# One fused two-block transformer kernel: order and queues of its first transfers, and zeros multiplied while x is loaded

## The reference

```python
h = rms_norm(x, norm_mix[l])
z = h @ w_in[l]
zu, zv, zq, zk, zval = jnp.split(z, cuts, axis=-1)
u = jax.nn.gelu(zu, approximate=False).reshape(Bn, Sn, SGU_GROUPS, SGU_CH)
v = jax.nn.gelu(zv, approximate=False).reshape(Bn, Sn, SGU_GROUPS, SGU_CH)
```

## Time and profile before

| what | value |
|---|---|
| median of 3 runs | 1712.66 us (1711.61 to 1713.93) |
| the profiled execution's own time | 1711.31 us |
| its span, first to last instruction | 1709.5 us |
| mean granted TensorE clock | 0.987 |
| busy: PE, DVE, ACT, POOL | 1586.1, 939.8, 690.7, 32.7 us |
| HBM read | 410.27 MB, 241 GB/s over the span |
| chain that ended last, by engine | PE 68%, DMA 21%, DVE 5%, ACT 4% |

### The profile page before, as it was taken

How to read it: one execution, slowest core, us unless ns; L and a number is a source line. 1 busy time by engine, 2 the same in 40 slices (tenths; PEclk the granted TensorE clock), 3 DMA queues, 4 the chain that set the end, 5 groups by cost and what they waited for, 6 DMA issues and landing times.

```text
span 1709.5 us, 30570 instructions
## 1 busy us (share of the span) xinstructions
PE 1586.1 (93%) x12545; PEld 1279.1 (75%) x12545; DVE 939.8 (55%) x1612; ACT 690.7 (40%) x1038; POOL 32.7 (2%) x42
## 2 busy tenths in 40 slices
PE   6999999787888887999999999999999999899999
PEld 5988876554555555788888678888788889678887
DVE  4887451011111111477667867676766677667766
ACT  5556451011001100444545465445545463754543
POOL 3000000000000000000000200000000000000000
PEclk9999999999999999999999999999999999999999
DMA  9744379999999999856464625564464653236460
GB/s 296 239 155 165 129 305 427 429 428 429 429 429 429 427 429 426 310 185 209 161 218 156 173 99 182 186 203 166 148 217 162 210 173 126 73 123 213 159 217 25
DMA packets 166637, 413.00 MB, mean 242 GB/s; under 512 B 5879, under 2 KB 131148, under 8 KB 154284
## 3 DMA queue, kind: packets, MB, share of 16 engines
q1 hardware_dynamic: 164512, 407.99, 64.0%
q0 software_dynamic: 1824, 4.03, 0.8%
q10 hardware_dynamic: 236, 0.06, 0.0%
HBM read 410.27 MB, written 1.78 MB: 241 GB/s over the span
## 4 chain that ended last, share of the span: by engine, by line
PE 68%; DMA 21%; DVE 5%; ACT 4%; issue 1%; SPq 0%; DVEq 0%; ACTq 0%
DMA odd_expert<-in_w_up_dram 19%; PE bank L1290 18%; PE bank L650 10%; PE bank L651 10%; PE bank L652 10%; PE bank L1294 9%; PE bank L1043 3%; DMA odd_expert<-in_w_gate_dram 2%; PE bank L1068 1%; ACT whi L1509 1%; DVE wlo L1979 1%; DVE x L2017 1%; PE bank L664 1%; PE bank L833 1%; PE bank L1057 1%
## 5 line engine op out<-in xcount | busy, mean ns | idle before, releaser
L1290 PE MATMUL bank<-x,whi 128*128 128x512 f32 x1408 | 356.4, 393 | 1.2 <-DVE x L2017 0.9
L1290 PEld LDWEIGHTS bank<-x,whi 128*128 128x128 f32 x1408 | 255.8, 189 | 50.9 <-issue 2.0
L2520 DVE TENSOR_TENSOR wlo<-raw,whi 128x2048 fp32r<-128x2048 f32 x120 | 271.4, 2289 | 32.6 <-ACT whi L1827 27.2
L1827 ACT ACTIVATE whi<-raw 128x2048 fp32r<-128x2048 f32 x120 | 225.4, 1913 | 57.9 <-PE bank L652 57.9
L1294 PEld LDWEIGHTS bank<-x,wlo 128*128 128x128 f32 x1408 | 193.7, 190 | 13.5
L1294 PE MATMUL bank<-x,wlo 128*128 128x256 f32 x1408 | 200.8, 282 | 0.0
L1979 DVE TENSOR_TENSOR wlo<-raw,whi 128x2048 fp32r<-128x2048 f32 x67 | 154.3, 2312 | 62.8 <-ACT whi L1509 62.2
L1509 ACT ACTIVATE whi<-raw 128x2048 fp32r<-128x2048 f32 x67 | 127.0, 1908 | 35.0 <-PE bank L652 29.3
L650 PE MATMUL bank<-whi,hh_hi 128*128 128x512 f32 x352 | 138.1, 392 | 3.1 <-DVE hh_lo L2505 3.1
L651 PE MATMUL bank<-whi,hh_lo 128*128 128x512 f32 x352 | 137.5, 391 | 0.0
L652 PE MATMUL bank<-wlo,hh_hi 128*128 128x512 f32 x352 | 137.0, 389 | 0.0
(11 more groups left out here) (351 smaller groups left out, 2302.9 us busy)
## 6 DMA issues: line engine op xcount, KB each, us to landing
raw<-in_ffn_w_gate_dram SPq DMA_DIRECT2D x44, 1024.0 KB, 5.4
raw<-in_ffn_w_up_dram SPq DMA_DIRECT2D x44, 1024.0 KB, 6.6
raw<-in_ffn_w_down_dram SPq DMA_DIRECT2D x44, 1024.0 KB, 6.2
raw<-in_w_gate_dram SPq DMA_DIRECT2D x16, 2048.0 KB, 20.9
raw<-in_w_up_dram SPq DMA_DIRECT2D x16, 2048.0 KB, 24.2
raw<-in_w_down_dram SPq DMA_DIRECT2D x16, 2048.0 KB, 24.4
odd_expert<-in_w_gate_dram SPq DMA_DIRECT2D x16, 2048.0 KB, 26.5
odd_expert<-in_w_up_dram SPq DMA_DIRECT2D x16, 2048.0 KB, 26.4
```

Source lines behind the costliest of these rows:

```text
L1290: pe.matmul(bank[:, :], hi[:, k, :], x_both[x][:, k, :, :].rearrange("p b n -> p (b n)"), start=k == 0, stop=False, skip_group_check=True)
L1827: act.activation(whi[:, c0_ % SPLIT, :], raw[:, c0_ % RAW, :], ACT.Copy).then_inc(hi_ready, 1)
L2520: dve.tensor_tensor(wlo[:, c0_ % SPLIT, :], raw[:, c0_ % RAW, :], whi[:, c0_ % SPLIT, :].bitcast(F32), ALU.subtract).then_inc(lo_ready, 1)
```

## The change

The table of constants is loaded in two pieces: the identity and the ones (columns 0 to 255, in front of weight chunk 0) and the rest (columns 256 to 1640, behind the rows of norm gains). The twelve DMAs of the norm gains are issued by SP behind chunk 0, and no longer by ScalarE. TensorE multiplies zeros twenty times before its first wait for data, and waits for the second piece of the constants (`in_c` at 32) after chunk 0.

```diff
@@ sync
             for tt in range(TT):
                 sp.dma_start(h[:, tt, :], ins["x"][0][tt * P:tt * P + P, :]).then_inc(in_x[tt], 16)
-            sp.dma_start(cst[:, :], consts).then_inc(in_c, 16)
+            sp.dma_start(cst[:, 0:C_BLK], consts[:, 0:C_BLK]).then_inc(in_c, 16)
...
             load_chunk(0)
+            at_row = [0]
+
+            def rows(dst, r0, src):
+                n = src.shape[0]
+                sp.dma_start(dst[r0:r0 + n, :], src).then_inc(in_rows, 16)
+                at_row[0] += 1
+
...
+            rows(rows_a, G_SGUB, ins["sgu_b"][0])
+            assert at_row[0] == 12
+            sp.wait_ge(in_c, 16)
+            sp.dma_start(cst[:, C_BLK:C_END], consts[:, C_BLK:C_END]).then_inc(in_c, 16)
             sp.wait_ge(in_rows, 16 * 12)
             sp.wait_ge(in_taps, 16 * 12)
             for c in range(1, moe_at):
@@ tensor
             pe.wait_ge(zero_ready, 1)
+            keep_busy(20, ps[1])
             pe.wait_ge(in_c, 16)
             pe.wait_ge(in_rows, 16 * 12)
...
             pe.wait_ge(in_taps, 16 * 12)
             pe.wait_ge(in_sgu, 16 * 4)
+            pe.wait_ge(in_c, 32)
             pe.wait_ge(cols_ready, 1)
@@ scalar
-            at_row = [0]
-
-            def rows(dst, r0, src):
-                n = src.shape[0]
-                act.dma_start(dst[r0:r0 + n, :], src).then_inc(in_rows, 16)
-                at_row[0] += 1
...
             act.wait_ge(in_c, 16)
             row_stats(h, ((in_x[0], 16), (in_x[1], 16)))
```

More of the change, by code:

```diff
@@ L479, in _ @@
             load_chunk(0)
+            at_row = [0]
[3 more added lines that the diff above has]
+                at_row[0] += 1
+            for r0, name in ((G_MIX, "norm_mix"), (G_XQ, "norm_xq"), (G_MEM, "norm_mem")):
+                rows(rows_a, r0, ins[name][0].rearrange("(k p) -> k p", p=P))
+            for r0, name in ((G_FFN1, "ffn1_norm_g_2"), (G_MIX2, "mix_norm_g_2"), (G_MEM2, "mem_norm_g_2"),
+                             (G_FFN2, "ffn2_norm_g_2")):
+                rows(rows_a, r0, ins[name].rearrange("l (k p) -> (l k) p", p=P))
+            rows(rows_a, G_KV, ins["kv_norm_g_2"].rearrange("(k p) -> k p", p=P))
+            for r0, name in ((G_LNG, "a_ln_g_2"), (G_LNB, "a_ln_b_2"), (G_DWB, "a_dw_bias_2")):
+                rows(rows_a, r0, ins[name][0].rearrange("(k p) -> k p", p=P))
+            rows(rows_a, G_SGUB, ins["sgu_b"][0])
+            assert at_row[0] == 12
+            sp.wait_ge(in_c, 16)
+            sp.dma_start(cst[:, C_BLK:C_END], consts[:, C_BLK:C_END]).then_inc(in_c, 16)
             sp.wait_ge(in_rows, 16 * 12)
@@ L1598, in used @@
                 act.wait_ge(chunk_used, c + 1)
-            at_row = [0]
-            def rows(dst, r0, src):
-                n = src.shape[0]
-                act.dma_start(dst[r0:r0 + n, :], src).then_inc(in_rows, 16)
-                at_row[0] += 1
-            for r0, name in ((G_MIX, "norm_mix"), (G_XQ, "norm_xq"), (G_MEM, "norm_mem")):
-                rows(rows_a, r0, ins[name][0].rearrange("(k p) -> k p", p=P))
-            for r0, name in ((G_FFN1, "ffn1_norm_g_2"), (G_MIX2, "mix_norm_g_2"), (G_MEM2, "mem_norm_g_2"),
-                             (G_FFN2, "ffn2_norm_g_2")):
-                rows(rows_a, r0, ins[name].rearrange("l (k p) -> (l k) p", p=P))
-            rows(rows_a, G_KV, ins["kv_norm_g_2"].rearrange("(k p) -> k p", p=P))
-            for r0, name in ((G_LNG, "a_ln_g_2"), (G_LNB, "a_ln_b_2"), (G_DWB, "a_dw_bias_2")):
-                rows(rows_a, r0, ins[name][0].rearrange("(k p) -> k p", p=P))
-            rows(rows_a, G_SGUB, ins["sgu_b"][0])
-            assert at_row[0] == 12
             act.wait_ge(in_c, 16)
```

## The result

The change made the kernel slower: 1716.46 us, median of 10 runs (1714.67 to 1719.77), against 1712.71 us (10 runs, 1710.85 to 1713.93) of the kernel before beside it. The ratio is 1.0025, 95% interval 1.0016 to 1.0034. The forecast was 1711.7 in a range from 1709.0 to 1714.0. The profiled execution took 1715.70 us, 4.39 more than that of before, with a span of 1713.9 us against 1709.5.

What follows compares the result with a forecast made beforehand. It took the opening's chain of waits, from the constants to TensorE's first weight matmul, as the bound. Of 2.9 us gained there, chunk 1 left 1.0: 1712.66 - 1.0 = 1711.7 us, range 1709.0 to 1714.0.

Steps and rivals of the forecast that it cites:

- The smaller first piece of the constants: Opening: first piece lands at 6.3, ScalarE starts 2.6 us sooner, and chunk 0 lands at 8.9 instead of 11.5.
- The gain rows on SP: Opening: twelve rows issued by SP land near 9.9, just behind chunk 0; the added issues are priced at zero.
- the opening: Up to the first weight matmul: TensorE starts chunk 0 at 14.2 to 14.5 instead of 17.17, 2.7 to 3.0 us sooner.
- The changed profile's own mark for wrong: Opening of the changed profile: TensorE starting chunk 0 later than 15 would show the forecast wrong.
- The zeros: Opening: twenty zero multiplications keep TensorE's rate up for the transposes, worth 0 to 0.3 us, taken as 0.2.
- Rival 4: Opening: zeros fail to keep TensorE's full rate until 9.9, taking back only 0.2 us; chance counted within the forecast's 0.50.
- nothing later gives it back or adds to it: After the first chunks: TensorE's gain there moves the rest of the program as a whole, unchanged.
- Chunk 1, the term that decides: At chunk 1: its issue stays at 12.35, landing at 17.45, so 1.0 us of the 2.9 gained is left.
- Rival 2: Before chunk 1: the rest of the constants delays the taps to 12.7, gain 0.5 us (1712.2); chance 0.15.
- Rival 3: SP's queue: SP's issue is held, last gain row issued at 14.1, chunk 1 3.3 us later (1716.0); chance 0.08.
- the gap of 1.5 to 2 us ahead of it: Near 20 us in the changed profile: TensorE waiting ahead of chunk 1, a sign that the forecast is right.
- Later transfers have room: After chunk 1: later loads stay in place; chunk 6's wlo ends at 46.27, TensorE needs it at 50.0 now.

Runs made afterwards that it cites:

- E1: The change without its twenty multiplications by zeros; 1712.54 us against 1713.38 for the kernel before, ratio 0.9996.
- E3: The kernel before with only the gain rows moved to SP behind chunk 0; 1714.40 us against 1713.38, ratio 1.0008.
- E9: The change without zeros, seven of the twelve gain rows on SP and five on ScalarE; 1712.13 us against 1713.75, ratio 0.9991.
- E2: The change with the twelve gain rows issued by ScalarE again; 1714.62 us against 1713.38 for the kernel before, ratio 1.0004.
- E7: The kernel before with only the constants split in two pieces; 1712.49 us against 1712.66, ratio 0.9990.
- E4: The kernel before with only the twenty multiplications by zeros added; 1716.02 us against 1713.38, ratio 1.0010.
- E5: The kernel before with twenty 8-column zero multiplications added in the opening; 1715.40 us against 1712.66, ratio 1.0010.
- E8: The kernel before with split constants and SP not waiting for the taps ahead of chunk 1; 1712.36 us against 1712.66, ratio 0.9992.
- E11: The kernel before with ten 8-column zero multiplications in the opening; 1714.06 us against 1713.75, ratio 1.0002.
- E12: The kernel before with split constants, no SP wait for taps, and 15 f32 zero multiplications in the opening; 1717.37 us against 1712.43, ratio 1.0025.
- E13: The whole change plus 108 8-column zero multiplications behind its twenty; 1714.03 us against 1712.31 for the kernel before, ratio 1.0010.
- E10: The kernel before with 128 8-column zero multiplications in the opening; 1715.34 us against 1713.75, ratio 1.0013.

## Why the prediction was wrong

**The smaller first piece of the constants**: right. ScalarE began at 6.12 (6.3 forecast), its squares at 6.23, chunk 0 landed at 9.8 (8.9 forecast: 7.7 us from its issue, where 6.8 were expected).

**The gain rows on SP**: this is the first step that failed. It priced the move at zero, with the rows "near 9.9, just behind chunk 0". They landed at 13.0. The sum took 2.5 us for a small transfer's way from chunk 1's row, and counted no time for twelve of them behind each other and behind 1 MB on one queue; E1, E3 and the change measure that at 2.6 to 3.2 us for twelve, E9 at 1.6 for seven. The step looked at when SP was free to issue, which was right and not the question. The rule quoted there, that issuing from several engines only saves issue time, is not what these runs show: with the same bytes in flight the rows land 1.8 to 2.7 us sooner on the other queue (E2 against the change, E7 against E1, before against E3). The Trainium skill has the reason for it in DMA: Bandwidth & Descriptors, Queues, rings and completion order: SP and ScalarE each have rings of their own, and each DMA engine takes turns between them; the trace agrees: in the kernel before, rows issued on ScalarE's queue up to 5.56 were all landed at 10.88, ahead of chunk 0 (11.5), which SP had issued at 2.1. With the rows at 13.0, **the opening** (14.2 to 14.5 forecast, 17.12 measured) lost its 2.7 us. The changed profile's own mark for wrong, TensorE starting chunk 0 later than 15, was the one that came true.

**The zeros**: "either way they end before the gain rows" held (8.45), and TensorE stood idle for 4.57 us behind them. They did keep the rate for a while: the granted clock is 1.00 from 6.7, where its record begins, to 13.5, and 0.50 from there to 16.9, so that the gain rows were turned in 0.29 us (0.43 before) and the 16 transposes took 3.26 us (3.57 before). Chunk 0 didn't gain by it. Rival 4, by which the rate is lost before, priced 0.2 and "nothing else"; that the zeros could cost something was in no step: "nothing later gives it back or adds to it" is the sentence that failed. Twenty multiplications were costed by their work and not as forty instructions that move all of TensorE's later code. That makes the late stop and what goes with it: the last expert takes 1.7 us (E4) and 1.5 us (E5) more with the order of the transfers left alone, and 3.3 in the change itself, out of 2.3, 2.6 and 4.0 us of the stretch. The sign of the result hangs on it: E1, without them, can't be told from the kernel before.

**Chunk 1, the term that decides**: mis-sized on the wrong side. It was issued at 13.26, not 12.35. The last head gain took 5.7 us; the bound given for full load was 4.8 plus half a microsecond. Rival 2 named the rest of the constants for such a delay. E7 has that piece too, issued sooner and with the rows on ScalarE, and issues chunk 1 at 12.39; E3 doesn't have it and issues at 13.82. So it is the rows again. Rival 3 had late rows too, but from another mechanism: its SP was held, and here all twelve were issued by 7.6. At chunk 1 itself the issue cost nothing, as chunk 0 was late anyhow: TensorE took chunk 1 up at 22.81, 0.07 us sooner than before where 1.0 was forecast, and the gap of 1.5 to 2 us ahead of it, named as a sign of being right, is missing. What the late issue cost came with chunk 6.

**Later transfers have room**: failed too. It compared chunk 6 with TensorE's need for it at 51.0, and not with what stands behind it on ScalarE, the norm of the memory tokens. The table of the fifteen traces shows it: chunk 6 decides at 280 as soon as it is taken up more than 20.2 us behind the end of chunk 0, and before had 19.3. There were 0.9 us of room, then, and chunk 6 came 2.0 us later in the change. E7 shows it without anything else wrong: 1.0 us gained at 21.84, 0.23 left at 280. The whole idea was therefore worth a quarter of a microsecond in a trace, and E7 and E8 are at ratios of 0.9990 and 0.9992 whose intervals reach 1.0000 and 1.0004.

**Rivals and range.** The range stopped at 1714.0 because the only slower case was rival 3 at half its price. A chance of 0.03 for slower had no room for a cost outside the opening.

Open is what makes chunk 0 run at the lower clock in some traces and not in others (E7 has an idle time of 0.88 us ahead of it and runs at the full rate, E8 with 1.24 us doesn't; the change with 0.72 us does, E9 with 0.72 us doesn't). Nor is it settled how much of the ±1 us by which chunk 6's landing differs is chance: E11 has the opening of before and takes chunk 6 up at 43.08. (It is taken up 29.7 to 30.7 us after chunk 1's issue in every trace but E12's, 31.7.) The medians are less regular than the stretches: E2 has the late stop and only 1.2 us more than the kernel beside it. And the kernel before itself took 1715.5 to 1718.1 us in 25 of its 135 executions on record, with most of the others between 1710 and 1714; that is as much as the late stop costs. No trace caught one of these, so it is open whether the same stop comes up there by chance. The placement of the code is shown by one trace for each kernel, by E4, E5 and E12 with nearly all of their executions above 1714.4, and by E13. No version here beats the kernel before by more than its measurement can tell.

## What to carry to other kernels

Ask of a moved DMA not only when it is issued but what stands ahead of it on its ring; a second queue is worth its cost for small transfers that something waits for. Look at everything queued on an engine behind a late load, not only at its consumer. And instructions added early, even idle ones, move all later code against the blocks in which it is fetched: run the same number of empty instructions as a control, and fill up to a whole block if the control costs what the change does. Last, a piece of "issue" on the chain is not yet a loss: compare the engine's own idle time at that place in both kernels.

## What the runs showed of the hardware that was not expected

- TensorE's code comes in as 16 KB packets on a queue of its own, 256 instructions each (E10 and E13: 256 instructions more, 48 packets instead of 47). At the last expert TensorE went on 2.4 to 2.6 us after the start of a packet that it waited for, in all fifteen traces, and was idle for 4.15 to 4.69 us ahead of that expert in each, the kernel before included.
- 40 early instructions brought a second stop of 0.73 to 2.17 us in four kernels of four (the change, E2, E4, E5), 60 one of 2.59 us (E12), and ten multiplications sooner. 20 and 256 brought none (E11, E10, E13).
- A short stop can cost more than itself: 0.73 us in the change came with 2.6 us of slower multiplication, since the clock stayed at its lower level for 10.2 us instead of 3.4. In E4 and E5 it was 0.1 and 0.2 us.
- Twelve DMAs of 2 to 8 KB landed 2.6 to 3.2 us behind a 1 MB transfer on the same queue (E1, E3, the change). On another queue they landed 0.1 to 0.7 us behind it (E2, E7, E8), and 0.7 us ahead of it in the kernel before.
- In the opening the view of the granted clock shows 1.00 where matmuls start 0.43 us apart, against 0.23 at the full rate (E8). The trace's record of the clock begins only at 20.3 us there, and at 16.1 in the kernel before; ahead of it the pace must be read instead.
